# Whole-row weight chunks and interleaved gate and up in a mixture-of-experts kernel

## The reference, cut to what matters

```python
def expert_block(args):            # xb: the rows routed to expert e
    xb, e = args
    hu = xb @ w_in[e]              # w_in[e]: 1024 x 1024, gate columns 0-511, up columns 512-1023
    return (jax.nn.silu(hu[:, :512]) * hu[:, 512:]) @ w_out[e]     # w_out[e]: 512 x 1024
```

## Time and profile before

| | us |
|---|---|
| median of 3 runs | 1376.23 |
| the runs | 1376.23, 1378.11, 1376.09 |
| span of the profiled execution, first to last instruction | 1378.2 |
| TensorE busy in it | 1279.1 |
| VectorE busy | 387.7 |
| ScalarE busy | 184.6 |
| bytes moved by DMA | 447.09 MB, 324 GB/s over the span |

### The profile page before, as it was taken

The page is one execution under the profiler, slowest core; times in us unless marked ns, Lnnn a source line. Parts: engine busy times, 40 slices in busy tenths (PEclk is TensorE's granted clock), DMA queues, the critical chain, the costliest instruction groups (busy, mean ns, idle before and its releaser), DMA issues.

```text
span 1378.2 us, 14140 instructions
## 1 busy us (share of the span) xinstructions
PE 1279.1 (93%) x5854; PEld 614.6 (45%) x5854; DVE 387.7 (28%) x572; ACT 184.6 (13%) x487; POOL 18.8 (1%) x23
## 2 busy tenths in 40 slices
PE   6949998999999999999999999899999999999997
PEld 5836655333444343333434455544334333444342
DVE  4318544223222222222222141422222223222222
ACT  1000011111111111111112131111111111111110
POOL 0000010000000000000000100000000000000000
PEclk9979998999999999999999999899999999999999
DMA  9865353799999999999999626398999999999995
GB/s 324 239 124 216 123 183 123 293 343 384 394 393 393 394 395 395 395 395 393 393 386 387 218 113 221 127 396 298 395 395 395 395 393 394 394 394 393 393 393 201
DMA packets 203718, 447.09 MB, mean 324 GB/s; under 512 B 16656, under 2 KB 19128, under 8 KB 203664
## 3 DMA queue, kind: packets, MB, share of 16 engines
q1 hardware_dynamic: 202688, 443.70, 86.5%
q0 software_dynamic: 976, 2.63, 1.3%
HBM read 443.68 MB, written 2.62 MB: 324 GB/s over the span
## 4 chain that ended last, share of the span: by engine, by line
PE 84%; DVE 4%; ACT 3%; issue 1%; DVEq 0%; ACTq 0%
PE ps L1000 83%; ACT work L488 2%; PE ps L1003 2%; DVE work L903 1%; DVE work L725 0%; DVE work L715 0%; DVE xs L937 0%; DVE work L643 0%; DVE work L710 0%; DVE work L708 0%; ACT work L478 0%; DVE work L896 0%; DVE work L726 0%; DVE xs L651 0%; DVE work L892 0%
## 5 line engine op out<-in xcount | busy, mean ns | idle before, releaser
L1000 PE MATMUL ps<-ring,work 128*64 128x512 f32 (+1 forms) x3456 | 855.2, 594 | 2.3 <-ACT work L478 1.5
L1000 PEld LDWEIGHTS ps<-ring,work 128*64 128x64 f32 (+1 forms) x3456 | 294.2, 144 | 521.6 <-issue 514.5
L1000 PE MATMUL ps<-work 128*128 128x128 f32 (+4 forms) x1730 | 320.9, 348 | 63.1 <-ACT work L488 24.1
L1000 PEld LDWEIGHTS ps<-work 128*128 128x128 f32 (+2 forms) x1730 | 224.2, 195 | 166.5 <-issue 109.4
L488 ACT ACTIVATE work<-ps,wcol 128x128 f32<-128x128 f32 x256 | 73.2, 368 | 327.3 <-PE ps L1000 327.3
L885 DVE RECIPROCAL work<-work 128x512 f32<-128x512 f32 x32 | 107.3, 3353 | 1.1
L883 DVE TENSOR_SCALAR work<-work 128x512 f32<-128x512 f32 x32 | 13.7, 428 | 332.1 <-ACT work L535 332.1
L903 DVE COPY work<-ps 128x256 f32<-128x256 f32 x32 | 13.6, 425 | 287.3 <-PE ps L1003 287.3
L535 ACT ACTIVATE work<-ps 128x512 f32<-128x512 f32 x32 | 19.1, 597 | 343.9 <-PE ps L1000 343.9
L543 ACT COPY work<-ps 128x512 f32<-128x512 f32 x64 | 37.5, 586 | 189.8 <-PE ps L1000 189.8
L1000 PE MATMUL ps<-work,ring 128*128 128x256 f32 x256 | 57.6, 388 | 1.3 <-DVE work L638 1.3
(11 more groups left out here) (110 smaller groups left out, 247.0 us busy)
## 6 DMA issues: line engine op xcount, KB each, us to landing
ring<-in_moe_w_in SPq DMA_DIRECT2D x120, 2048.0 KB, 17.5
ring<-in_moe_w_out SPq DMA_DIRECT2D x60, 2048.0 KB, 18.9
ring<-in_hg_w_in SPq DMA_DIRECT2D x7, 2048.0 KB, 20.6
work<-in_moe_w_in SPq DMA_DIRECT2D x4, 2048.0 KB, 9.0
ring<-in_moe_w_in SPq DMA_DIRECT2D x8, 1024.0 KB, 14.7
ring<-in_moe_w_out SPq DMA_DIRECT2D x8, 1024.0 KB, 14.4
ring<-in_w_kv SPq DMA_DIRECT2D x4, 2048.0 KB, 19.7
ring<-in_hg_w_out SPq DMA_DIRECT2D x2, 2048.0 KB, 11.7
```

The costliest lines, as they stand in the source:

```text
L1000: return pe.matmul(o, l, r, start=start, stop=stop)
```

## The change

A chunk of gate and up becomes a row half instead of a column half. Partition p now holds rows 8p to 8p+7 of w_in[e]: four of them, all 1024 columns, in the first chunk and four in the second, each chunk one run of 16 KB per partition. A down chunk holds rows 4p to 4p+3 of w_out[e], also 16 KB in one run. To match, hn and hid are written permuted (feature 8p+k into block k, and 4p+k for hid), and ffn_norm is needed in that order too (wrow, beside wcol, which the router still reads). Since each chunk has parts of both gate and up, TensorE accumulates both banks over the first chunk and then both over the second: gate, up, gate, up, 16 instructions each. A new semaphore, rows_done, marks the first chunk as read. In the last pair the second chunk comes in two parts, and each is worked off as gate, up. Each first pair waits for both gathered halves at its start.

```diff
@@ views
+        hn_rows = region(0).rearrange("p (a k q) -> p a q k", k=KD, q=P)
+        hid_rows = hid.rearrange("p (k q) -> p q k", k=KF)
...
+        def rows_view(c):
+            return c.rearrange("p (k n) -> p k n", n=2 * FF)
+        def rows_of(w, half):
+            return w.rearrange("(p k) n -> p k n", k=KD)[:, half * (KD // 2):(half + 1) * (KD // 2), :]
+        def down_rows(w):
+            return w.rearrange("(p k) n -> p k n", k=KF)
@@ SP
                 q = layer * PAIRS + r // 6
+                if r % 6 < 2:
+                    return rows_done, it * UN + (q + 1)
                 if r % 6 < 4:
-                    return up_done, it * (2 * UN) + (2 * q + 1 + r % 6 // 2)
+                    return up_done, it * (2 * UN) + (2 * q + 2)
...
             for l in range(2):
+                sp.dma_start(wrow[:, l, :], ffn_norm[l].rearrange("(p k) -> p k", k=KD)).then_inc(late_in, 16)
                 sp.dma_start(wcol[:, 3 + l, :], ffn_norm[l].rearrange("(k p) -> p k", p=P)).then_inc(late_in, 16)
...
-                    copy(up_view(c), cols(moe_w_in[layer, e], j // 2))
+                    copy(rows_view(chunk(c)), rows_of(moe_w_in[layer, e], j // 2))
                 else:
-                    copy(down_view(c), moe_w_out[layer, e].rearrange("(k p) n -> p k n", p=P))
+                    copy(down_view(c), down_rows(moe_w_out[layer, e]))
...
-                                    ks = slice(part * (KD // 2), (part + 1) * (KD // 2))
-                                    dst, src = up_view(c + x2)[:, ks, :], cols(moe_w_in[layer, e], 1)[:, ks, :]
+                                    ks = slice(part * (KD // 4), (part + 1) * (KD // 4))
+                                    dst = rows_view(chunk(c + x2))[:, ks, :]
+                                    src = rows_of(moe_w_in[layer, e], 1)[:, ks, :]
@@ ACT, weighted_columns
-                                       scale=wcol[:, 3 + layer, 4 * half + k:4 * half + k + 1])
+                                       scale=wrow[:, layer, 4 * half + k:4 * half + k + 1])
@@ DVE, norm and silu
-                dve.tensor_scalar(dst[:, a, :], xs[:, a, :], rstd[:, a:a + 1], None, ALU.mult).then_inc(xn_ready, 1)
+                dve.tensor_scalar(dst, src, rstd[:, a:a + 1], None, ALU.mult).then_inc(xn_ready, 1)
+            def norm_rows(i, a, meanwhile=lambda: None):
+                norm(i, hn, hn_rows[:, a], xs[:, a, :].rearrange("p (q k) -> p q k", k=KD), a, meanwhile)
...
-                    dve.tensor_tensor(hid, en, ps[:, 7, :], ALU.mult).then_inc(hid_ready, 1)
+                    dve.tensor_tensor(hid_rows, en.rearrange("p (q k) -> p q k", k=KF),
+                                      ps[:, 7, :].rearrange("p (q k) -> p q k", k=KF), ALU.mult).then_inc(hid_ready, 1)
@@ PE
-            def up(weights, bank, buf, signal, ks=range(KD)):
+            def up(weights, half, buf, gate_up, ks):
                 for k in ks:
                     for x2 in range(2):
                         rows = slice(x2 * BLK, (x2 + 1) * BLK)
-                        i = mm(ps[rows, bank, :], xgT[:, buf, k, rows], weights[x2][:, k, :], k == 0, k == KD - 1)
+                        i = mm(ps[rows, 6 + gate_up, :], xgT[:, buf, 4 * half + k, rows],
+                               weights[x2][:, k, gate_up * 512:(gate_up + 1) * 512],
+                               half == 0 and k == 0, half == 1 and k == KD // 2 - 1)
...
-                            if not n0:
-                                pe.wait_ge(y_ready, it * (2 * UN) + (2 * q - 1 + half))
-                            if first and half == 0:
-                                pe.wait_ge(nblk_ready, layer + 1)
-                                up(w, 6, 0, None, range(KD // 2))
-                                pe.wait_ge(xg_ready, 2 * q + 2)
-                                up(w, 6, 0, up_done, range(KD // 2, KD))
-                            elif last and half:
-                                up(w, 7, u % 2, None, range(KD // 2))
+                            if half == 0:
+                                if first:
+                                    pe.wait_ge(nblk_ready, layer + 1)
+                                    pe.wait_ge(xg_ready, 2 * q + 2)
+                                for gate_up in range(2):
+                                    if not n0:
+                                        pe.wait_ge(y_ready, it * (2 * UN) + (2 * q - 1 + gate_up))
+                                    i = up(w, 0, u % 2, gate_up, range(KD // 2))
+                                i.then_inc(rows_done, 1)
+                            elif last:
+                                up(w, 1, u % 2, 0, range(KD // 4))
+                                up(w, 1, u % 2, 1, range(KD // 4))
                                 arrived(ring_chunk(layer, r, it), it)
                                 arrived(ring_chunk(layer, r + 1, it), it)
-                                up(w, 7, u % 2, up_done, range(KD // 2, KD))
+                                for gate_up in range(2):
+                                    up(w, 1, u % 2, gate_up, range(KD // 4, KD // 2)).then_inc(up_done, 1)
                             else:
-                                up(w, 6 + half, u % 2, up_done)
+                                for gate_up in range(2):
+                                    up(w, 1, u % 2, gate_up, range(KD // 2)).then_inc(up_done, 1)
```

More of the change, by code:

```diff
@@ L76, in build @@
         wcol = sb("wcol", [P, 5, KD])
+        wrow = sb("wrow", [P, 2, KD])
         lbl = sb("lbl", [P, 2, H])
@@ L212, in gate_or_up @@
             c = extra[r - RING] if in_extra(r, it) else chunk(ring_chunk(layer, r, it))
-            return c.rearrange("p (k n) -> p k n", n=512)
+            return rows_view(c)
         def up_view(c):
@@ L329, in load_next @@
                     if in_extra(r, it):
-                        load_expert(layer, r, gate_or_up(layer, r, it), cols(moe_w_in[layer, 2 + r % 2], 1), it)
+                        load_expert(layer, r, gate_or_up(layer, r, it), rows_of(moe_w_in[layer, 2 + r % 2], 1), it)
                     else:
@@ L362, in load_last @@
                                     dst = down_view(c + x2)[:, :, ns]
-                                    src = moe_w_out[layer, e].rearrange("(k p) n -> p k n", p=P)[:, :, ns]
+                                    src = down_rows(moe_w_out[layer, e])[:, :, ns]
                                     part_in = down_part_in
@@ L639, in transposed, with norm @@
                                       ALU.mult).then_inc(hT_dve, 1)
-            def norm(i, dst, a, meanwhile=lambda: None):
-                link(dve.tensor_tensor_reduce(out=dst[:, a, :], in0=xs[:, a, :], in1=xs[:, a, :], scale=1.0,
+            def norm(i, junk, dst, src, a, meanwhile=lambda: None):
+                link(dve.tensor_tensor_reduce(out=junk[:, a, :], in0=xs[:, a, :], in1=xs[:, a, :], scale=1.0,
                                               scalar=0.0, op0=ALU.mult, op1=ALU.add, accum_out=ms[:, a:a + 1]))
                 rms(i + a, a, a + 1, D, meanwhile)
-                dve.tensor_scalar(dst[:, a, :], xs[:, a, :], rstd[:, a:a + 1], None, ALU.mult).then_inc(xn_ready, 1)
+                dve.tensor_scalar(dst, src, rstd[:, a:a + 1], None, ALU.mult).then_inc(xn_ready, 1)
+            def norm_rows(i, a, meanwhile=lambda: None):
+                norm(i, hn, hn_rows[:, a], xs[:, a, :].rearrange("p (q k) -> p q k", k=KD), a, meanwhile)
             def add_projection(n, a, half):
@@ L657, in projected_and_normed @@
                 add_projection(n, 0, 1)
-                norm(i, hn, 0)
+                norm_rows(i, 0)
                 transposed((2, 6)[n], 0, 0, [(hrT, 3 + n)])
@@ L854, in over @@
                             dve.wait_ge(s["sil"], v)
-                            dve.tensor_tensor(hid, en, ps[:, 7, :], ALU.mult).then_inc(s["hid"], 1)
+                            dve.tensor_tensor(hid_rows, en.rearrange("p (q k) -> p q k", k=KF),
+                                      ps[:, 7, :].rearrange("p (q k) -> p q k", k=KF), ALU.mult).then_inc(s["hid"], 1)
                             dve.wait_ge(s["ht"], v)
@@ L1133, in up @@
                         rows = slice(x2 * BLK, (x2 + 1) * BLK)
-                        i = mm(ps[rows, bank, :], xgT[:, buf, k, rows], weights[x2][:, k, :], k == 0, k == KD - 1)
-                if signal is not None:
-                    i.then_inc(signal, 1)
+                        i = mm(ps[rows, 6 + gate_up, :], xgT[:, buf, 4 * half + k, rows],
+                               weights[x2][:, k, gate_up * 512:(gate_up + 1) * 512],
+                               half == 0 and k == 0, half == 1 and k == KD // 2 - 1)
+                return i
             def hidden_T(bank, signal):
@@ L1171, in over @@
                             pe.wait_ge(s["w"], v * (16 * 6))
-                            up((up_view(0), up_view(1)), 6, 0, None)
-                            up((up_view(2), up_view(3)), 7, 0, s["up"])
```

(7 more changed lines are left out.)

7 lines of the change are left out of this document (5 added, 2 removed).

## The result

The changed kernel takes 1397.74 us (median of 4 runs, 1397.13 to 1398.45), the kernel before, beside it on the same chip, 1377.17 (4 runs, 1376.09 to 1378.98). The ratio is 1.0148 with a 95% interval of 1.0134 to 1.0162: slower by 20.6 us, between 18.4 and 22.3. The forecast was 1392.6, in a range of 1385 to 1404.

A forecast was written before the change was run, and what follows sets the result against it. TensorE was taken as the bound, never stopping for a weight. Terms 6.8 (later gate) + 6.0 (clock) + 2.6 (first pairs) + 1.0 (small loads) = 16.4 us, on 1376.2 gave 1392.6; range 1385 to 1404.

The forecast's parts named there:

- Part 1: Weight transfers: runs of 16 KB should be no slower, 400 to 430 GB/s expected; worth 0 us.
- Part 2: Full pairs: gate is complete later, but the new TensorE stop replaces the old 0.80 us one; 0 for each of 30.
- its own test: Sign set beforehand: the forecast is wrong if the period of a pair, 30.75 us, changes by over 0.1 us.
- part 7: Permuted writes of hn and hid, neighbouring elements 512 bytes apart: taken as 0; for hid, bounds 0 and +0.53 us.
- Part 3: Last pair of each layer: gate is complete later with no gather to cover it; 3.38 us each, 6.8 in all.
- Part 4: Last pairs: TensorE's clock falls around the 4.2 us idle stretch and slows later work; 3.0 us each, 6.0 in all.
- The rival that the clock stays: Last pairs: the clock does not fall, the idle stretch being too short; time 1386.6 us, chance 12%.
- Part 5: First pair of each layer: it now waits for both gathered halves; 2.6 us in all, bounds 2.4 and 5.
- Part 6: Opening: two more small wrow loads in SP's queue delay VectorE's release; 1.0 us, bounds 0 and 10.
- the 96 to 100 that the forecast had set itself: Sign set beforehand: the forecast is wrong if VectorE is released from the small vectors before 96 or after 100.
- the rival's 1399: Permuted hid write 0.37 us slower, delaying transposes: 5.7 us in full pairs, 0.7 in last ones; time 1399, chance 27%.

The follow-up runs named there:

- order-only run: Changed kernel with its layout, small loads and 16 KB runs, but gate over both row halves first, then up, as before: 1377.74 us, ratio 1.0001.
- layout-only run: Changed kernel with down chunks back in 4 KB runs and the product with up written to neighbouring elements: 1392.39 us, ratio 1.0112.
- the dummies: Changed kernel plus ten unused matmul instructions into a free bank while TensorE waits in each last pair: 1394.80 us, ratio 1.0126.

## Why the prediction was right, point by point

- **Part 1**, right: faster transfers and no time for them; the order-only run shows it.
- **Part 2**, right for the order alone: the layout-only run keeps 30.75. In the changed kernel the step fails by its own test, a period changed by over 0.1 us (0.12), and the cause is the term of part 7.
- **Part 3**, right: in a last pair the product with up starts 17.48 after the pair's first instruction, not 14.06: 3.42 against 3.38.
- **Part 4**, right: 2.84 in each last pair against the 3.0 put in, shown by the dummies. The rival that the clock stays fell: 4.6 us were enough.
- **Part 5**, right, 2.8 for 2.6, but not the same in both layers: 1.11 in layer 0, where the gather before it took 6.36 and not 6.64, and 1.69 in layer 1.
- **Part 6**, mis-sized: 1.0 put in, none found. The release of VectorE at 94.93 also lies outside the 96 to 100 that the forecast had set itself.
- **Part 7**, mis-sized, the one step that matters: 0 put in for the product with up, 0.35 us found (its upper bound of 0.53, one ns for each of 512 elements, comes to 0.51). The rows of writes with every second element, which I went by, did not speak for writes 512 bytes apart; L788, which pointed the right way, was the better row. The rival had the price (0.37) and the mechanism: second half of the gather at 17.36 (17.43 seen), 5.7 us in full pairs and 0.7 in last ones (0.7). In full pairs 3.6 were seen: the second half comes 0.26 later in the pair shown and 0.18 later in others (318.92 - 301.57 against 319.68 - 302.51), and then takes 1.95 for 2.05. For hn the 0 held: its write grew by 0.6 us, and VectorE's wait ahead of the router step shrank from 1.29 to 0.69. The rule on lines of 16 bytes in "Advanced Engine Details and Errata" of the Trainium skill, set aside in the forecast, agrees with this trace in sign; the size, 1031 ns for 687, is the run's.

So parts 3, 4 and 5 make 6.8 + 5.7 + 2.8 = 15.3 of the 19.3 us found (15.4 forecast), and the longer product 4.3, less the 0.3 between the layers. (The layout-only run gained 5.4, since in it the low clock also fell less on work; whether the shorter product brought that is open.) Two misses ran against each other by luck, the 1.0 of part 6 that did not come and the 4.3 that nothing was put in for. The time lies 5 us above the forecast, within its range, between its case and the rival's 1399.

## What to carry to other kernels

When an order is changed to finish an intermediate later, look first for the place where no other work stands behind it: 30 covered pairs lost nothing to the order, two uncovered ones 12.5 us, almost half of that as clock. Make longer DMA runs only where a transfer is waited for, and count what the layout that they force costs the engines. An idle gap is better filled by moving real work into it: here the same blocks in another order gave 8 us alone, and 22 once the gate and up chunks came in longer runs, which had been worth nothing before.

## What the runs showed of the hardware

- A VectorE product of 128x512 fp32 took 0.69 us with neighbouring outputs and 1.03 to 1.05 with outputs 512 bytes apart; a scaling of 128x1024, 0.75 and 1.32 to 1.37.
- Four TensorE transposes took 0.60 us from neighbouring elements and 0.67 from every fourth.
- In short stretches with its engines full, one core's DMA moved 387 GB/s in 2 KB runs, 403 in 4 KB, and 423 and 437 in 16 KB ones.
- In the last pairs the low clock showed behind stops of 4.6, 2.69, 1.18 (32 down instructions in 8.52 and 8.78 us) and once 0.85 us (8.78), and did not behind others of 1.19 and 0.85 (7.09). It need not take a stop of 4 us, and the length of the stop alone did not decide.
- At the start of layer 1, where a 16 KB packet of TensorE's instructions falls, TensorE went on 2.2 to 2.7 us after its wait for the residual had ended. With nine transposes ahead of that place 1.0 to 1.5 us of it were a stop; with none, all of it (about 2.5). A gain that ends there can be lost.
